# A macaron layer step on one core: FFN 1's first result tile kept in SBUF, the vector engine's setup and low parts in another order, and the samples' state products in four parts inside the tenth gate unit

## The chip, the cores and the metric

The kernel runs on one core of one Trainium2 chip. The metric is the device time of one launch in microseconds. The kernel before took 2427.97 us (median of 3 runs, 2427.48 to 2428.36).

## The reference, cut to what matters

One decoder layer step for 1024 prompt tokens and 8 sample tokens (1032 columns in all), all in float32, model width 1024:

```
x = x + 0.5 * (silu(n1 @ W_gate) * (n1 @ W_up)) @ W_down     # FFN 1, n1 = rmsnorm(x), inner width 2816
proj  = rmsnorm(x) @ w_in            # RWKV features | S5 input u | 2048 columns of gates
y_a   = rwkv7(features, state)       # matrix-state recurrence, 8 heads of 64
y_b   = s5(u, state)                 # bu = ug @ bb; x_t = ab * x_{t-1} + bu_t; y = x @ C + D * u; GELU; GLU
x = x + (sigmoid(g_a) * (y_a @ w_a_up) + sigmoid(g_b) * (y_b @ w_b_up)) @ w_out
x = x + 0.5 * FFN 2(rmsnorm(x));  outputs: rmsnorm(x), last features, RWKV and S5 states
```

## The kernel before

All activations lie with the model width on the 128 partitions and the 1032 tokens along the free axis, in 8 tiles. Every float32 operand of a large product is split into a high part (`whi`, `b11_hi`, ...) and a low part (`wlo`, ...), and a product is three matmuls, high by high, high by low and low by high.

**FFN 1, first half.** The inner width 2816 is 22 tiles of 128 rows. Gate and up of one tile together are a *pair* (`NP` = 22, numbered 0 to 21). A pair is done as seven Strassen products, n = 0 to 6, of 24 matmuls each (4 weight tiles, 3 parts, 2 column blocks of 258) on the seven operands b11, t1, t2, b21, t3, b22, t4, which stay in SBUF (L939 for a pair, L902 for one product). ScalarE (ACT) makes the high parts of the weights (L749) and copies some products out of PSUM (L849, L855, L861); GpSimd (POOL) makes sums of weight parts (L504) and the low parts (L501); VectorE (DVE) adds, scales by `rstd` and multiplies (L663 to L686). The last DVE step of a pair (named `a2`, L686; L644 for pairs 0 and 1) leaves the pair's result, a *tile* of 128 x 1032, in `gate[:, j]`, j = pair mod 2. SyncE (SP) then stores it to DRAM (`spill`, L414).

PE waits in each pair for a few of these steps: product 2 for ACT's first copy (`p1`), product 5 for ACT's third copy (`p5`, L861), product 6 for DVE's `u2a` (L668); and every product for the low part of its weights (`st_lo`, L501).

**FFN 1, second half ("down").** 4 blocks of tiles (0 to 5, 6 to 11, 12 to 17, 18 to 21) times 8 output tiles are 32 *units* of up to 54 matmuls of 344 columns (L983). A unit needs the high and low parts of its block's result tiles. These go through 18 *slots* of SBUF (`g.slot`), most of which overlap the seven operands and so come free only when a product of the last pair has read its operand for the last time. SP brings a tile back (`a_back`, L457), ACT makes its high part (`tile_high`, L830), DVE its low part (`tile_low`, L651). Slot 15, that of tile 0, lies over x's last two rows, which are used up after pair 0. Unit 0 is done in two pieces: tiles 0 to 2 when DVE's `g2a` of pair 21 is there (L675), tiles 3 to 5 when `u1` is there (L681). DVE adds the first piece at L696, and each unit at L703; PE's unit u waits until unit u - 2 has been added. POOL splits the weights of each unit (L542, L544).

All engines run their own instruction streams in order: an instruction that waits holds up all that stand behind it on that engine. SP's queue is in order too: `spill(20)`, `a_back(0)`, weights of units 0 and 1, `a_back(1)` to `a_back(5)` (each pair of them behind a product of pair 21), 8 loads of x, `spill(21)`, weights of unit 2, `a_back(6)` and so on.

**The S5 setup.** DVE computes the S5 tables in the gaps: a generator of some 600 small instructions (`s5_setup_dve`, L1122 on), of which `spend` (L1256) issues a share behind each pair (slot number below 22, nominally 4700 ns) and behind each down unit (slot 22 + u, nominally 2700 ns). Four table parts (`turn`) come first, then short instructions on 128 x 16 values, then the parts `in` and `out`. ACT stores a finished part in a later slot.

**The projection stage.** 16 gate units (L206, 8 weight tiles of 9 matmuls of 344 columns) have the S5 products between them: `to_state` (L1873), `out` (L1903, L1907), and after gate unit 8 `samples` (L1884), 64 matmuls of 8 columns in one run.

Of the kernel before, what the change touches and what calls it, by code (L numbers as in the profile page):

```python
# [15 lines left out]
NB = 8  # L16
TOK = SEQ + NB
DT = D // P
# [329 lines left out]
def first_ffn(nc, g, w_up, w_down, gcol, gnext, x_in, x_rows, consts_in, s5_in, a_dram, x_dram, setup, ahead, block):  # L348
# [6 lines left out]
    spilled = [16, 16]  # L355
# [51 lines left out]
    def _(sp):  # L407
# [31 lines left out]
        spill(0, 0, 0)  # L439
# [24 lines left out]
        a_back(0, 15)  # L464
# [84 lines left out]
    def _(v):  # L549
# [86 lines left out]
        for j in range(2):  # L636
# [7 lines left out]
            on(v.tensor_tensor(gate, gate, up, ALU.mult))  # L644
# [9 lines left out]
        for pair in range(2, NP):  # L654
# [3 lines left out]
            if last:  # L658
                for t in range(4):
                    tile_low(t)  # L660
# [7 lines left out]
            on(v.tensor_tensor(U[1], two("x", j), U[1], ALU.add))  # L668
            g.fst_up.wait(v, 0, pair, "u2a")
            on(v.tensor_tensor(U[1], U[1], R[1], ALU.mult))  # L670
            if last:
                tile_low(4)
# [5 lines left out]
            if last:  # L678
                tile_low(5)
            done(v, 0, pair, 6)  # L680
            on(v.tensor_tensor(U[0], two("x", j), R[0], ALU.mult))  # L681
            g.fst_up.wait(v, 0, pair, "u1")
# [3 lines left out]
            on(v.tensor_tensor(G[1], G[1], U[1], ALU.mult))  # L686
            if not last:
                setup["vector"](pair, PAIR_NS)
                assert pair < NP - 2 or setup["tables"]() == 4
        for u in range(len(FIRST_BLOCKS) * DT):  # L690
            b, k = divmod(u, DT)
            xd = blocks(g.xd[:, k, :])
            if u == 0:
                v.wait_ge(g.x_in[0], 32)
                v.wait_ge(g.m_half, 1)
                v.scalar_tensor_tensor(xd, g.ps[:, 5:8, 0:BLK], 0.5, xd, ALU.mult, ALU.add).then_inc(g.set_free[1], 1)  # L696
# [19 lines left out]
    def _(act):  # L716
# [109 lines left out]
        def tile_high(t):  # L826
            b, k = divmod(t, 6)
            act.wait_ge(g.a_in[t % 6], 16 + 16 * (t // 6 + 1))
# [3 lines left out]
        for pair in range(2, NP):  # L832
# [15 lines left out]
            act.wait_ge(g.a_out[j], spilled[j] + 16 * (pair // 2))  # L848
# [24 lines left out]
            if pair == NP - 2:  # L873
                tile_high(0)
# [376 lines left out]
def s5_setup(g, s5_dram):  # L1251
# [294 lines left out]
def s5_block(nc, g, w_gate, w_glu, w_b, gate_dram, wb_dram, o_dram, cs_dram, x0_in, y_dram, ys_dram, s5p_out, s5s_out,  # L1546
# [25 lines left out]
    if block:  # L1572
# [280 lines left out]
        def _(pe):  # L1853
# [3 lines left out]
            def gate(k):  # L1857
                product(pe, g, 0, 0, u0 + k, DT, k % 2, use[k % 2] + k // 2, 0, hi, lo, None, inside.get(k))
# [18 lines left out]
            def samples(y_turns):  # L1877
                pe.wait_ge(g.v_free, 4)
                pe.wait_ge(g.y_set, 2 * y_turns)
                for n in range(2):  # L1880
                    for j in range(J):
                        for q in range(2):
                            c = (n * J + j) * NB
                            last = pe.matmul(g.ps[rows(q), 6, c:c + NB], g.G8[:, j, n, rows(q)],  # L1884
# [2378 lines left out]
```

## Time and profile before

| | |
|---|---|
| profiled execution | 2429.68 us, span 2427.9 us, TensorE clock 0.992 of full speed |
| PE busy | 2367.0 us (97%) |
| DVE, POOL, ACT busy | 1390.5, 1186.2, 711.5 us |
| DMA | 243.89 MB, mean 100 GB/s |

PE is at work nearly all the time. The span in 40 slices of some 61 us shows where it is not: in the first slice, in the eighth (`PE ...9 8...`, `PEld ...7...`, from 425 us), around slices 21 to 26, where the recurrence runs, and in the last one. The chain that ended last reaches back only to 1573.65 us and is 32% PE; before that the order of the stages is told by PE's own idle times. "PEld" is the weight load of TensorE, which overlaps the matmuls. The clock column of the window view is the granted TensorE clock, 1.00 being 2.4 GHz.

### The profile page before, as it was taken

How to read it: one execution, taken by the hardware profiler on the slowest of the kernel's cores; microseconds unless marked ns; L12 is line 12 of the kernel's file. 1: busy time of each engine (PE TensorE's matmuls, PEld its weight loads, DVE VectorE, ACT ScalarE, POOL GpSimd, SP SyncE). 2: the span in 40 equal slices, each digit the busy share in tenths (PEclk: the TensorE clock that was granted, in tenths of full speed). 3: DMA queues.
4: the chain of work that ended last, by engine and by line, in shares of the span. 5: the costliest groups of instructions: out<-in, count | busy, mean ns of one | idle time of the engine just before them, and what ended most of it. 6: DMA issues, size and time to landing. Idle time of an engine off the chain costs nothing. (4 is left out here: it accounts for less than half of the span.)

```text
span 2427.9 us, 51909 instructions
## 1 busy us (share of the span) xinstructions
PE 2367.0 (97%) x21964; PEld 2310.3 (95%) x21964; DVE 1390.5 (57%) x2023; ACT 711.5 (29%) x1349; POOL 1186.2 (49%) x750
## 2 busy tenths in 40 slices
PE   8999999899999999999989999999999999999997
PEld 8999999799999999999988888899999999999997
DVE  6666666788545455652566676576844444453225
ACT  6333333311020000111437666312433333341001
POOL 3868686634434345322330000254777777765640
PEclk9999999999999999999999999999999999999999
DMA  5212121344333523634360110172222222153212
GB/s 215 94 63 94 70 104 70 139 171 133 99 104 136 114 88 108 153 86 129 131 203 18 34 33 4 50 260 87 79 87 76 79 74 81 61 196 95 82 46 71
DMA packets 104135, 243.89 MB, mean 100 GB/s; under 512 B 17240, under 2 KB 43480, under 8 KB 103328
## 3 DMA queue, kind: packets, MB, share of 16 engines
q1 hardware_dynamic: 76560, 190.72, 23.8%
q10 hardware_dynamic: 27408, 50.76, 6.6%
q8 instruction: 126, 2.06, 0.4%
q14 instruction: 41, 0.34, 0.1%
HBM read 174.47 MB, written 65.82 MB: 99 GB/s over the span
## 5 line engine op out<-in xcount | busy, mean ns | idle before, releaser
L172 POOL TENSOR_TENSOR whi<-wraw,small 128x1024 fp32r<-128x1024 f32 (+1 forms) x60 | 103.3, 1721 | 417.2 <-PE ps L206 340.7
L206 PE MATMUL ps<-hhi,whi 128*128 128x344 f32 x816 | 176.9, 325 | 0.0
L206 PE MATMUL ps<-hlo,whi 128*128 128x344 f32 x816 | 173.1, 320 | 0.0
L206 PE MATMUL ps<-hhi,wlo 128*128 128x344 f32 x816 | 172.8, 320 | 0.0
L909 PE MATMUL ps<-t_hi,whi 128*128 128x258 f32 x672 | 138.1, 287 | 12.3 <-POOL wlo L501 5.7
L175 POOL TENSOR_TENSOR wlo<-wraw,whi 128x1024 fp32r<-128x1024 f32 (+1 forms) x60 | 145.5, 2424 | 4.7
L3939 PE MATMUL ps<-t_hi,whi 128*128 128x258 f32 x704 | 143.6, 285 | 3.1 <-ACT ffn_gate L3846 1.0
L3939 PE MATMUL ps<-t_lo,whi 128*128 128x258 f32 x704 | 142.1, 283 | 0.0
L3939 PE MATMUL ps<-t_hi,wlo 128*128 128x258 f32 x704 | 141.2, 282 | 0.0
L206 PEld LDWEIGHTS ps<-hhi,whi 128*128 128x128 f32 x816 | 136.3, 189 | 2.1 <-issue 0.7
L206 PEld LDWEIGHTS ps<-hlo,whi 128*128 128x128 f32 x816 | 137.9, 189 | 0.0
L909 PE MATMUL ps<-t_lo,whi 128*128 128x258 f32 x672 | 137.2, 286 | 0.0
L206 PEld LDWEIGHTS ps<-hhi,wlo 128*128 128x128 f32 x816 | 136.7, 188 | 0.0
L909 PE MATMUL ps<-t_hi,wlo 128*128 128x258 f32 x672 | 136.4, 285 | 0.0
L2218 POOL TENSOR_TENSOR sm_v<-sm_v,rw_e 128x2048 f32<-128x2048 f32 x1 | 3.6, 3622 | 256.1 <-DVEq L1981 256.1
L909 PE MATMUL ps<-b_hi,whi 128*128 128x258 f32 x576 | 117.5, 286 | 8.7 <-DVE b_lo L561 8.7
L909 PEld LDWEIGHTS ps<-t_hi,whi 128*128 128x128 f32 x672 | 105.2, 192 | 15.1 <-POOL wlo L501 8.6
L3622 POOL TENSOR_TENSOR wlo<-weights_sum,whi 128x512 fp32r<-128x512 f32 x66 | 92.3, 1399 | 52.5 <-ACT whi L3818 51.3
L909 PE MATMUL ps<-b_lo,whi 128*128 128x258 f32 x576 | 116.8, 284 | 0.0
L501 POOL TENSOR_TENSOR wlo<-weights_sum,whi 128x512 fp32r<-128x512 f32 x60 | 86.0, 1433 | 63.1 <-ACT whi L749 62.4
L909 PE MATMUL ps<-b_hi,wlo 128*128 128x258 f32 x576 | 116.1, 283 | 0.0
L983 PE MATMUL ps<-a_hi,whi 128*128 128x344 f32 x528 | 112.0, 320 | 1.7 <-issue 1.5
(592 smaller groups left out, 6823.9 us busy)
## 6 DMA issues: line engine op xcount, KB each, us to landing
weights_raw_b<-ffn_up SPq DMA_DIRECT2D x22, 1024.0 KB, 5.0
wraw<-ffn_up SPq DMA_DIRECT2D x21, 1024.0 KB, 5.0
a_spilled<-ffn_gate SPq DMA_DIRECT2D x40, 516.0 KB, 2.7
a_raw<-a_spilled SPq DMA_DIRECT2D x40, 516.0 KB, 4.3
wraw<-ffn_down SPq DMA_DIRECT2D x48, 384.0 KB, 3.2
wraw<-w_mix SPq DMA_DIRECT2D x18, 512.0 KB, 3.6
gates<-gate_out ACTq DMA_DIRECT2D x16, 516.0 KB, 3.5
wraw<-w_gates SPq DMA_DIRECT2D x16, 512.0 KB, 3.9
```

The source lines that it names most:

```text
L172: pool.tensor_tensor(g.whi[:, s, 0:n], g.wraw[:, s, 0:n], g.zero.to_broadcast([P, n]), ALU.add).then_inc(g.w_hi, 1)
L175: pool.tensor_tensor(g.wlo[:, s, 0:n], g.wraw[:, s, 0:n], g.whi[:, s, 0:n].bitcast(F32), ALU.subtract).then_inc(g.w_split, 1)
L206: last = pe.matmul(g.ps[:, 3 * bank_set + b, 0:BLK], w[:, s, k * P:(k + 1) * P], x(k, b), start=(k == 0 and first), stop=(k == kt - 1 and ...
L501: pool.tensor_tensor(ring(g.wlo, n), source(n), ring(g.whi, n).bitcast(F32), ALU.subtract).then_inc(g.st_lo, 1)
L909: last = pe.matmul(g.ps[:, b0 + c, 0:QB], w(k), x[:, k, c * QB:(c + 1) * QB], start=start and k == 0 and fresh, stop=k == DT // 2 - 1 and ...
L983: last = pe.matmul(g.ps[:, b0 + c, 0:BLK], w[:, s, n * P:(n + 1) * P], x[:, c * BLK:(c + 1) * BLK], start=n == tiles[0] and fresh, stop=n ...
L2218: st.do(pool.tensor_tensor(V, V, over(E7[:, :, sample]), ALU.mult))
L3622: pool.tensor_tensor(ring(g.wlo, n), source(n), ring(g.whi, n).bitcast(F32), ALU.subtract).then_inc(g.st_lo, 1)
L3939: last = pe.matmul(g.ps[:, b0 + c, 0:QB], ring(w, r, k), x[:, k, c * QB:(c + 1) * QB], start=start and k == 0 and first, stop=k == DT // 2 ...
```

## The change

1. **Tile 0 stays in SBUF.** Pair 0's last multiply (L644) writes straight into slot 15 instead of `gate[:, 0]`, after waiting that the first operands and `t4`'s low part are made. `spill(0)` and `a_back(0)` are gone. ACT makes the tile's high part after pair 3 instead of after pair 20, DVE its low part after pair 4 instead of in pair 21. ACT's first copy in pair 2 waits for pair 0's last multiply instead of for the spill.
2. **Low parts in pair 21.** DVE made tiles 0 to 3 ahead of the pair's steps, 4 after `u2m`, 5 after `g2m`. Now it makes 1 and 2 ahead, 3 between `u2a` and `u2m`, and 4 and 5 after `u1`, followed by the addition of unit 0's first piece, which stood behind the pair's two last multiplies.
3. **Setup.** `spend` stops in the pairs once the four table parts are done (after pair 18), and goes on in the down units.
4. **Samples.** The 64 small matmuls are issued 16 at a time behind weight tiles 0 to 3 of gate unit 9 instead of all behind unit 8.

```diff
@@ first_ffn, SP
-        spill(0, 0, 0)
         spill(0, 0, 1)
...
-        a_back(0, 15)
@@ first_ffn, DVE
-            on(v.tensor_tensor(gate, gate, up, ALU.mult))
+            if j == 0:
+                v.wait_ge(g.b_hi, HI0)
+                v.wait_ge(g.t4_lo, 4)
+                on(v.tensor_tensor(g.slot[15][2][:, :], gate, up, ALU.mult))
+            else:
+                on(v.tensor_tensor(gate, gate, up, ALU.mult))
...
             if last:
-                for t in range(4):
-                    tile_low(t)
+                tile_low(1)
+                tile_low(2)
...
+            if pair == 4:
+                tile_low(0)
@@ first_ffn, ACT
-            act.wait_ge(g.a_out[j], spilled[j] + 16 * (pair // 2))
+            if pair == 2:
+                g.fst_up.wait(act, 0, 0, "a2")
+            else:
+                act.wait_ge(g.a_out[j], spilled[j] + 16 * (pair // 2))
...
-            if pair == NP - 2:
+            if pair == 3:
                 tile_high(0)
@@ s5_setup
     def spend(slot, ns):
+        if slot < NP and len(ready) == 4:
+            return
...
                 ready.append(slot)
+                if slot < NP and len(ready) == 4:
+                    return
@@ gate units, PE
-            def samples(y_turns):
+            def samples(k):
+                if k >= 4:
+                    return
+                if k == 0:
+                    pe.wait_ge(g.v_free, 4)
+                    pe.wait_ge(g.y_set, 2 * 6)
+                for x in range(2 * J // 4 * k, 2 * J // 4 * (k + 1)):
+                    n, j = divmod(x, J)
...
+                if k == 3:
+                    last.then_inc(g.v_done, 1)
```

The rest of the diff counts semaphores anew, one spill and one load fewer.

ACT at the turn from pair 20 to pair 21, before. `a_hi_212` is the high part in slot 15 (tile 0), `a_raw_214` the tile as loaded, L844 the silu, L749 the weights' high parts, L849 the first copy:

```order
L844 ACTIVATE ffn_gate<-ffn_gate 128x516
L830 ACTIVATE a_hi_212<-a_raw_214 128x1032
L749 ACTIVATE whi<-weights_sum 128x512
L849 ACTIVATE ffn_gate<-ps 128x516
L749 ACTIVATE whi<-weights_raw_b 128x512
L855 ACTIVATE ffn_up<-ps 128x516
```

The same place after (L854 the silu, L756 the high parts, L862, L868 and L874 the three copies, L840 `tile_high`; `a_hi_167` and `a_hi_170` are tiles 1 and 2):

```order
L854 ACTIVATE ffn_gate<-ffn_gate 128x516
L756 ACTIVATE whi<-weights_sum 128x512
L862 ACTIVATE ffn_gate<-ps 128x516
L756 ACTIVATE whi<-weights_raw_b 128x512
L868 ACTIVATE ffn_up<-ps 128x516
L756 ACTIVATE whi<-weights_raw_b 128x512
L840 ACTIVATE a_hi_167<-a_raw_169 128x1032
L840 ACTIVATE a_hi_170<-a_raw_172 128x1032
L874 ACTIVATE ffn_gate<-ps 128x516
L756 ACTIVATE whi<-weights_sum 128x512
```

Tile 0 no longer stands between pair 20's silu and pair 21's weights; tiles 1 and 2 stand, as before, between pair 21's second and third copy.

DVE in pair 21, before (L651 `tile_low`, L663 to L681 the pair's steps):

```order
L651 TENSOR_TENSOR a_lo_213<-a_raw_214,a_hi_212 128x1032
L651 TENSOR_TENSOR a_lo_168<-a_raw_169,a_hi_167 128x1032
L651 TENSOR_TENSOR a_lo_171<-a_raw_172,a_hi_170 128x1032
L651 TENSOR_TENSOR a_lo_174<-a_raw_175,a_hi_173 128x1032
L663 TENSOR_TENSOR ffn_gate<-ps,ffn_gate 128x516
L665 TENSOR_TENSOR ffn_gate<-ffn_gate,rstd 128x516
L668 TENSOR_TENSOR ffn_up<-ps,ffn_up 128x516
L670 TENSOR_TENSOR ffn_up<-ffn_up,rstd 128x516
L651 TENSOR_TENSOR a_lo_177<-a_raw_178,a_hi_176 128x1032
L675 TENSOR_TENSOR ffn_gate<-ps,ffn_gate 128x516
```

DVE at the turn from pair 20 to pair 21, after (L692 and L694 the two last multiplies of pair 20, L654 `tile_low`):

```order
L692 TENSOR_TENSOR ffn_gate<-ffn_gate,ffn_up 128x516
L694 TENSOR_TENSOR ffn_gate<-ffn_gate,ffn_up 128x516
L654 TENSOR_TENSOR a_lo_168<-a_raw_169,a_hi_167 128x1032
L654 TENSOR_TENSOR a_lo_171<-a_raw_172,a_hi_170 128x1032
L666 TENSOR_TENSOR ffn_gate<-ps,ffn_gate 128x516
```

No setup instruction stands behind pair 20 any more, and two low parts instead of four stand ahead of pair 21's steps.

PE around gate unit 9, before (L206 a gate unit's matmuls, L1884 the samples):

```order
L206 MATMUL ps<-hhi,wlo 128x344 x3
L1884 MATMUL ps<-s_u,s_to_state 64x8 x64
L206 MATMUL ps<-hhi,whi 128x344 x3
L206 MATMUL ps<-hlo,whi 128x344 x3
L206 MATMUL ps<-hhi,wlo 128x344 x3
```

After (L1904 the samples):

```order
L1904 MATMUL ps<-s_u,s_to_state 64x8 x16
L206 MATMUL ps<-hhi,whi 128x344 x3
L206 MATMUL ps<-hlo,whi 128x344 x3
L206 MATMUL ps<-hhi,wlo 128x344 x3
L1904 MATMUL ps<-s_u,s_to_state 64x8 x16
```

The run of 64 has become four runs of 16 with 9 large matmuls between them.

## Rows read from the trace of the kernel before

**Rows 1.** Windows: us, busy time (instructions) by engine, granted clock, DMA.

```profile
300.00:420.00 120.00, 119.70 (x993) 119.08 (x993) 80.92 (x166) 41.46 (x72) 92.12 (x66) 1.00 0.24 88
...
465.30:470.60 5.30, 5.28 (x24) 5.28 (x25) 3.50 (x2) 1.99 (x3) 5.30 (x3) 0.50 0.44 181
...
1092.20:1095.60 3.40, 3.40 (x16) 3.38 (x15) 2.38 (x6) 0.00 (x0) 0.65 (x1) 0.52 0.77 238
```

**Rows 2.** Timeline, PE, FFN 1's last two pairs: start, length, instruction, idle before.

```profile
449.22 0.51 PE L909 MATMUL ps<-t_hi,whi 128*128 128x258 f32 x2 [3.81 <-DVE ffn_up L668]
...
465.32 0.80 PE L909 MATMUL ps<-t_hi,whi 128*128 128x258 f32 x2 [5.67 <-POOL wlo L501]
...
484.60 0.71 PE L983 MATMUL ps<-a_hi,whi 128*128 128x344 f32 x3 [1.52 <-issue]
```

**Rows 3.** Timeline, DVE: end of pair 18, setup behind pair 19.

```profile
409.50 0.69 DVE L686 TENSOR_TENSOR ffn_gate<-ffn_gate,ffn_up 128x516 f32<-128x516 f32 x1
...
432.32 1.27 DVE L1177 TENSOR_TENSOR s_par<-vec 128x16 f32<-128x16 f32 x1
...
446.85 0.17 DVE L1199 TENSOR_SCALAR s_par<-s_par 128x16 f32<-128x16 f32 x1
```

**Rows 4.** Timeline, ACT: the high parts of tiles 0, 1 and 2.

```profile
461.73 1.06 ACT L830 ACTIVATE a_hi<-a_raw 128x1032 fp32r<-128x1032 f32 x1 [9.46 <-DMA a_raw<-a_spilled]
462.70 0.61 ACT L749 ACTIVATE whi<-weights_sum 128x512 fp32r<-128x512 f32 x1
...
465.23 2.07 ACT L830 ACTIVATE a_hi<-a_raw 128x1032 fp32r<-128x1032 f32 x2
```

**Rows 5.** Timeline, SP's queue (the length is from first to last).

```profile
432.57 23.74 SPq L414 DMA_DIRECT2D a_spilled<-ffn_gate  x2
456.41 0.40 SPq L457 DMA_DIRECT2D a_raw<-a_spilled  x1
...
458.18 15.94 SPq L457 DMA_DIRECT2D a_raw<-a_spilled  x5
```

**Rows 6.** Tile a_raw, 440 to 540 us: low parts in ns, loads to landing.

```profile
L651 DVE TENSOR_TENSOR a_lo<-a_raw,a_hi x11: 1223/1236/2889, 462.9 to 533.3; 128x1032 fp32r<-128x1032 f32 x11
...
DMA to landing us min/median/max: 3.4/5.6/8.7
```

**Rows 7.** Timeline, DVE: pair 21 and the first down units.

```profile
476.83 0.68 DVE L663 TENSOR_TENSOR ffn_gate<-ps,ffn_gate 128x516 f32<-128x516 f32 x1
...
490.44 1.23 DVE L696 SCALAR_TENSOR_TENSOR x_down<-ps,x_down 128x1032 f32<-128x1032 f32 x1
493.86 1.23 DVE L703 SCALAR_TENSOR_TENSOR x_down<-ps,x_down 128x1032 f32<-128x1032 f32 x1 [2.19 <-PE ps L983]
...
507.00 1.23 DVE L703 SCALAR_TENSOR_TENSOR x_down<-ps,x_down 128x1032 f32<-128x1032 f32 x1
```

**Rows 8.** Timeline, POOL: weights of units 0, 2 and 5 (5 waits for unit 3).

```profile
480.62 2.19 POOL L544 TENSOR_TENSOR wlo<-wraw,whi 128x768 fp32r<-128x768 f32 x1
...
497.59 1.85 POOL L544 TENSOR_TENSOR wlo<-wraw,whi 128x768 fp32r<-128x768 f32 x1
...
519.38 1.57 POOL L542 TENSOR_TENSOR whi<-wraw,small 128x768 fp32r<-128x768 f32 x1 [5.06 <-PE ps L983]
```

**Rows 9.** Timeline, PE: the samples between gate units 8 and 9.

```profile
1087.80 0.63 PE L206 MATMUL ps<-hhi,wlo 128*128 128x344 f32 x3
1088.36 3.99 PE L1884 MATMUL ps<-s_u,s_to_state 128*64 128x8 f32 x128
1092.28 1.23 PE L206 MATMUL ps<-hhi,whi 128*128 128x344 f32 x3
```

**Rows 10.** Page, part 5: POOL's low parts of the pairs' weights (mean ns).

```profile
L501 POOL TENSOR_TENSOR wlo<-weights_sum,whi 128x512 fp32r<-128x512 f32 x60 | 86.0, 1433 | 63.1 <-ACT whi L749 62.4
```

**Rows 11.** Timeline of pair 2, POOL and PE.

```profile
65.16 2.25 POOL L501 TENSOR_TENSOR wlo<-weights_sum,whi 128x512 fp32r<-128x512 f32 x1
...
67.52 0.48 PE L909 MATMUL ps<-t_hi,whi 128*128 128x258 f32 x2 [1.33 <-ACT ffn_gate L849]
```

More of the change, by code:

```diff
@@ L354, in first_ffn @@
     x_late = [*g.a_in, *g.a_out]
-    spilled = [16, 16]
+    spilled = [0, 16]
     def raw(par):
@@ L668, in _ @@
             on(v.tensor_tensor(U[1], two("x", j), U[1], ALU.add))
+            if last:
+                tile_low(3)
             g.fst_up.wait(v, 0, pair, "u2a")
             on(v.tensor_tensor(U[1], U[1], R[1], ALU.mult))
-            if last:
-                tile_low(4)
             done(v, 0, pair, 5)
@@ L677, in _ @@
             on(v.tensor_tensor(G[1], G[1], R[1], ALU.mult))
-            if last:
-                tile_low(5)
             done(v, 0, pair, 6)
             on(v.tensor_tensor(U[0], two("x", j), R[0], ALU.mult))
+            if last:
+                tile_low(4)
+                tile_low(5)
+                xd = blocks(g.xd[:, 0, :])
+                v.wait_ge(g.x_in[0], 32)
+                v.wait_ge(g.m_half, 1)
+                v.scalar_tensor_tensor(xd, g.ps[:, 5:8, 0:BLK], 0.5, xd, ALU.mult, ALU.add).then_inc(g.set_free[1], 1)
             g.fst_up.wait(v, 0, pair, "u1")
@@ L827, in tile_high @@
             b, k = divmod(t, 6)
-            act.wait_ge(g.a_in[t % 6], 16 + 16 * (t // 6 + 1))
+            if t == 0:
+                g.fst_up.wait(act, 0, 0, "a2")
+            else:
+                act.wait_ge(g.a_in[t % 6], 16 + 16 * (t // 6 + (t % 6 > 0)))
             hi, _, full = g.slot[FIRST_BLOCKS[b][2][k]]
@@ L847, in _ @@
             done(act, 0, pair, 0)
-            act.wait_ge(g.a_out[j], spilled[j] + 16 * (pair // 2))
+            if pair == 2:
+                g.fst_up.wait(act, 0, 0, "a2")
+            else:
+                act.wait_ge(g.a_out[j], spilled[j] + 16 * (pair // 2))
             on(act.activation(G[0], two("x", j), ACT.Copy))
@@ L1857, in gate @@
             def gate(k):
-                product(pe, g, 0, 0, u0 + k, DT, k % 2, use[k % 2] + k // 2, 0, hi, lo, None, inside.get(k))
+                product(pe, g, 0, 0, u0 + k, DT, k % 2, use[k % 2] + k // 2, 0, hi, lo, None, inside.get(k),
+                        samples if k == SAMPLE_UNIT else None)
             def to_state(p, y_turns):
@@ L1875, in to_state @@
                 last.then_inc(g.v_done, 1)
-            def samples(y_turns):
[L1878 to L1884, printed above, removed]
-                                             g.U8[:, 2 * j + q, NB + CH:CH + 2 * NB], start=True, stop=True)
-                last.then_inc(g.v_done, 1)
+            def samples(k):
[6 more added lines that the diff above has]
+                    n, j = divmod(x, J)
+                    for q in range(2):
+                        last = pe.matmul(g.ps[rows(q), 6, x * NB:x * NB + NB], g.G8[:, j, n, rows(q)],
+                                         g.U8[:, 2 * j + q, NB + CH:CH + 2 * NB], start=True, stop=True)
+                if k == 3:
+                    last.then_inc(g.v_done, 1)
             def out(p, w, states):
@@ L1912, in _ @@
                      4: [lambda: to_state(2, 2)], 5: [lambda: out(1, 0, 3)], 6: [lambda: to_state(3, 4)],
-                     7: [lambda: out(2, 0, 4)], 8: [lambda: samples(6)], 9: [lambda: out(3, 0, 5)]}
+                     7: [lambda: out(2, 0, 4)], 9: [lambda: out(3, 0, 5)]}
+            SAMPLE_UNIT = 9
             inside = {4 + 2 * p: (6, lambda p=p: out(p, 1, 0)) for p in range(4)}
@@ L3262 @@
 M0, S0, T0 = 16, 4, 4
-DONE0, IN0, OUT0 = 7 * NP, 8 * NP, 16 + 8 * NP
-BACK0 = [16 + 16 * len(range(r, FT, 6)) for r in range(6)]
+DONE0, IN0, OUT0 = 7 * NP, 8 * NP, (8 * NP, 16 + 8 * NP)
+BACK0 = [16 * (r > 0) + 16 * len(range(r, FT, 6)) for r in range(6)]
 SPILLED = NP - KEPT
@@ L3842, in body @@
                 if b < 10 and (b or j >= 2):
-                    act.wait_ge(g.a_out[j], i * 16 + (OUT0 + 16 * b))
+                    act.wait_ge(g.a_out[j], i * 16 + (OUT0[j] + 16 * b))
                 if b == 10:
```

5 lines of the change are left out of this document (1 added, 4 removed).

## The prediction

> **What bounds the kernel now.** I read the page's busy times and its 40 slices first: PE is busy 97% of the span, so only PE's idle or slowed time can be won, and the change can pay only where PE waits today. The window view then gives two kinds of stretches. In a steady one PE is full: 993 matmuls in 120 us [rows 1], so one matmul takes 0.1208 us and a product of 24 takes 2.90 us. The turn from FFN 1's first half to its second is the other kind. PE's timeline [rows 2] shows it in one column, the idle time before an instruction. Product 6 of pair 20 starts at 449.22 after 3.81 us, so product 5 was over at 445.4; product 2 of pair 21 at 465.32 after 5.67 us, and the first down unit at 484.60 after 1.52 us. The clock adds to it: after each long idle time the granted clock is the lower level, 1.2 GHz; the 24 matmuls from 465.3 to 470.6 took 5.3 us at 0.50 [rows 1]. From 445.4 to 484.6 eight products were done; at 2.90 us each they need 23.2 us. The stretch lost 39.2 - 23.2 = 16.0 us, which is nearly all that this part of the change can win.
>
> Who was late? For the first stall, DVE: its setup behind pair 19 runs from 432.32 to 447.02 [rows 3], three times its nominal 4.7 us, and the step for which PE waits (L668) stands behind it. For the second, ACT: it sat 9.46 us in front of tile 0's high part [rows 4], with pair 21's weight split behind it, because SP could load tile 0 (456.41) only after its in-order `spill(20)` (the second of the two at 432.57, issued at its end, 456.31), which waited for the same late DVE [rows 5]. So both stalls have one root, DVE, and one amplifier, tile 0 in ACT's order.
>
> **The stretch after the change.** Without setup behind pair 19, DVE does its steps as products end, and both stalls go. Products then end back to back: pair 20's last at 448.3, pair 21's products 0 to 6 at 451.2, 454.1, 457.0, 459.9, 462.8, 465.7 and 468.6. What is late next has to be followed along each engine.
>
> *SP and the DMA.* Pair 18, whose DVE steps run without a delay, ends its last one at 410.19 [rows 3]. Its last product ended 14 products, 40.6 us, before pair 20's 448.3, at 407.7, so 2.5 us earlier. For pair 20 that gives 450.8. `spill(20)` goes then, the weights of units 0 and 1 by 452.0, `a_back(1)` and (2) at about 452.1 and 452.5, (3) and (4) at 454.2, (5) at 460.0. Tile 1 before: issued at 458.18, taken by ACT at 465.23 at once, so landed within 7.0 us [rows 4, 5], tile 2 a little later; both lie between the minimum and the maximum of 3.4 and 8.7 [rows 6]. One tile of 0.53 MB (tile 0) is gone from the queue ahead of them, 1.3 us at the 400 GB/s of a full queue. So tile 1 lands near 457.8 and tile 2 near 458.8.
>
> *ACT.* Its two high parts (2.07 for two [rows 4]) end near 459.8; its third copy, at the 0.6 of a piece of 512 columns (row at 462.70 [rows 4]), at 460.4, the weights of product 5, as long, at 461.0, POOL's low part (1.43 on average [rows 10]) at 462.4. PE wants product 5 at 462.8. This holds by 0.4 us only: I cost it at nothing and keep it as the first rival.
>
> *DVE.* Low parts of tiles 1 and 2 end between 461.5 and 462.3. From there to `g2a`, for which the first down unit waits, stand exactly the six instructions that stood there before, in another order: five steps and one low part. They took from 476.83 [rows 7] to just before PE's start at 484.60 [rows 2], 7.7 us, and the low part alone has the longest row of its kind, 2.89 [rows 6]. So the down stage starts at 462.0 + 7.7 = 469.7 at the middle. POOL's weights for unit 0 ended at 482.81 [rows 8], 6.4 us after product 4's end (470.6 plus two products, 476.4), so now at 469.2: not later than DVE.
>
> PE therefore starts down at 469.7 instead of 484.60: **14.9 us won**. Bounds: 16.0 if nothing is late; 11.4 if the loads land 3.5 us later than I say.
>
> The Trainium skill (page "SBUF — State Buffer", section "Who interferes with whom") says that a DVE instruction with two SBUF inputs and a GpSimd instruction that reads SBUF exclude each other for a whole instruction. The trace agrees: the same low part takes between 1.22 and 2.89 us [rows 6], the long ones while POOL worked. With no such exclusion the low part would take 1.23, DVE would not be the limit, and the sum would be 0.5 us better.
>
> **The down stage.** The two last multiplies of pair 21 now stand behind two low parts and the first addition. Before, that addition began 5.8 us after the start of down (490.44 [rows 7]) and the multiplies were over by then; now I get 8.5 us. `spill(21)`, the weights of unit 2 and `a_back(6)` are queued behind it on SP, 2.6 us later against PE. Unit 2's weights were ready at 499.44 [rows 8], 2.9 us before PE wanted them (unit 0 over at 493.8 [rows 7], one more of 8.5: 502.3), and the 8 loads of x, which crowded them, will have landed: I cost this at nothing, 0 to 1 us.
>
> The setup that is taken out of the pairs, 3 + 27 + 20 instructions, comes behind the units: slots 0 to 2 now hold some 15 short ones each. A unit takes 8.5 us (unit 0 over at 493.8 [rows 7], unit 3 at 519.3 [rows 8]); DVE has an addition of 1.23, a low part of 1.23 to 2.9, and 15 instructions of 0.2 us, of which about three may wait for POOL's 3.4 us per unit: 5.5 to 9 us. Unit 1's addition ran from 507.00 to 508.2 [rows 7], 2.6 us before PE needed its banks at 510.8 (two units after 493.8). In the sum nothing; it is the second rival. The setup then ends four units later, near unit 21, before DVE gets its second job in the last block.
>
> In unit 0 an idle time of 0.17 us goes: 0.1.
>
> **Pair 2.** ACT's wait for the spill is replaced by one for a multiply that ends earlier. PE idled 1.33 us there, but POOL's low part for the same product ended at 67.41, 0.1 us before PE started [rows 11]. Won: 0.1, bounds 0 and 1.3. The high and low part of tile 0 (1.06 and 1.23 us) fall into pairs 3 and 4, in which ACT and DVE have idle time and PE has none.
>
> **Samples.** 128 recorded small matmuls take from 1088.36 to 1092.28 [rows 9], and the 3.4 us behind them run at 0.52 of the clock [rows 1]. At full clock that work takes 1.8, so 1.6 us can be won if the clock stays up. Each change between small and large costs: three large ones issued from 1087.80 take 0.48, so 0.1 goes by until 1088.36; for coming out, where a full weight load follows a short matmul, I estimate twice that. Three more of each are 0.8 us. Net 0.8 won. No row shows small and large ones mixed like this, so bounds are 1.6 won and 1.4 lost (the clock falls all the same, and the changes cost twice as much). DVE's wait for the result moves into a gap of 10 us.
>
> **Sum:** 14.9 + 0.1 + 0.1 + 0.8 = 15.9 us. The profiled execution took 2429.68 us (span 2427.9 and 1.8 around it): 2413.8. The median shown, 2427.97, is 1.7 lower, so I predict 2412.1.
>
> **Rivals.** *ACT still stands in front of a load.* Tiles 1 and 2 land as late as the latest load before, 8.7 us after issue: 461.2, so product 5 waits some 2 us; if the stall grows to 3 or 4 us, the lower clock costs another 1.5 to 2.5, as at 465. The total gain is then 10 to 12: 2416 to 2418, say 2417. For it: 0.4 us of margin. Against it: a shorter queue.
>
> *Setup crowds the units.* Behind pair 19, 27 instructions took 14.7 us, 0.54 each [rows 3]. If the 15 short ones of a slot do the same, a unit costs DVE 8.1 + 2.5 to 4.1 = 10.6 to 12.2 us against 8.5; over three units 6 to 11, less the 2.6 of slack: 3.5 to 8.5 us of stalls. Then 2415.5 to 2420.5, say 2418. Against it: POOL works 3.4 us of 8.5 there, and worked nearly always behind pair 19.
>
> *The same, and slower than before.* If each of the short ones waits for one POOL instruction, 1.2 us as at 432.32 [rows 3], a slot costs 20.5 us, three of them 61.5 against 25.5: 33 us lost after slack, and the time is about 2445. Slower begins where a short one costs more than 0.82 us on average ((25.5 + 2.6 + 16) / 3 = 14.7 for a slot, less 2.5, over 15).
>
> *The samples lose.* The clock falls and the changes cost double: 2.2 us worse than forecast, 2414.3. This is inside the forecast's own range.
>
> **How the numbers follow.** Forecast (own range 2410 to 2415.5) 0.62; ACT behind a load 0.17; crowded units, mildly 0.10; both or more, ending near no change, 0.06; slower 0.05. For 8 in 10: 2409.5 to 2419. The lower end is all bounds at once, 16.0 + 0.1 + 1.3 + 1.6 = 19 us, slightly cut. A change under 0.2% (4.9 us) can't be told from none. Faster by more 0.89, within 0.06, slower 0.05.
>
> **What would show it.** In the new trace PE has no idle time between 430 and 468 us and keeps the full clock; one short wait for DVE's `g2a` before the first down unit near 469.7; ACT's idle time before its first high part in pair 21 under 4 us. Behind the samples the clock stays at 2.4 GHz and unit 9 ends 0.8 us earlier against unit 8's end. I am wrong if PE waits for POOL's weights at product 5, or for DVE's additions in units 3 to 5.

## The result, and the profile after

The changed kernel takes 2415.76 us (median of 5 runs, 2415.53 to 2417.57) against 2428.36 for the kernel before (5 runs, 2427.48 to 2429.63): ratio 0.9949, 95% interval 0.9936 to 0.9962, 12.6 us less. The forecast was 2412.1, with a range of 2409.5 to 2419 for 8 in 10; its narrower range, 2410 to 2415.5, was missed by 0.3 us. One of the 19 runs of the kernel before beside the first experiments took 8030.62 us and does not count in their ratios. The profiled executions are 14.1 us apart, 2429.68 and 2415.58.

Where these 14.1 us come from is read from one kind of event, DVE's reads of finished units and gate tiles, which both traces have: how much earlier does each come? At 50 us it is 0.2 us already, before anything that the change touches has a part in it; at the first down unit 12.60 (read on PE); in DVE's addition of unit 0 12.99, and again 12.99 from unit 8 to 968 us; at gate unit 4 of the projection 13.67; at unit 9 14.34; at the end 14.1. The additions of units 1 to 7 come only 9.4 to 12.4 us earlier, since DVE runs behind there, but PE is not held up by it. So 12.4 us were won at the turn (12.60 less the 0.2) and 0.4 in unit 0. Another 0.7 appeared in the first gate units, where the change does nothing, and 0.67 at the samples.

The windows of the changed kernel (columns as in [rows 1]) show a steady stretch as full as before, the turn without a slow clock, and a stretch over the second and third of the samples' four parts:

```profile
300.00:420.00 120.00, 119.70 (x994) 119.08 (x993) 79.43 (x163) 41.28 (x72) 92.27 (x66) 1.00 0.25 88
430.00:459.00 29.00, 28.89 (x241) 28.69 (x240) 9.11 (x11) 9.47 (x17) 22.39 (x16) 1.00 0.31 111
461.60:464.60 3.00, 2.93 (x24) 2.93 (x25) 2.41 (x3) 2.37 (x3) 1.35 (x1) 1.00 0.34 125
1079.00:1082.60 3.60, 3.60 (x72) 3.35 (x69) 1.51 (x5) 0.00 (x0) 0.19 (x1) 1.00 0.80 256
```

PE's idle times at the turn, to be held against [rows 2]. The waits of 3.81 and 5.67 us are gone. A new one stands before product 4 of pair 21 (461.67), and the first down unit starts at 472.00:

```profile
461.67 0.51 PE L922 MATMUL ps<-t_hi,whi 128*128 128x258 f32 x2 [2.05 <-ACT ffn_gate L874]
467.88 0.51 PE L922 MATMUL ps<-t_hi,whi 128*128 128x258 f32 x2 [0.20 <-POOL wlo L499]
472.00 0.74 PE L996 MATMUL ps<-a_hi,whi 128*128 128x344 f32 x3 [0.96 <-POOL wlo L542]
```

ACT there ([rows 4] before), with L840 the high parts of tiles 1 and 2, L874 the third copy and L756 the weights of product 5:

```profile
458.71 1.06 ACT L840 ACTIVATE a_hi<-a_raw 128x1032 fp32r<-128x1032 f32 x1 [3.71 <-DMA a_raw<-a_spilled]
459.99 1.06 ACT L840 ACTIVATE a_hi<-a_raw 128x1032 fp32r<-128x1032 f32 x1 [0.21 <-DMA a_raw<-a_spilled]
460.96 0.58 ACT L874 ACTIVATE ffn_gate<-ps 128x516 f32<-128x516 f32 x1
461.44 0.62 ACT L756 ACTIVATE whi<-weights_sum 128x512 fp32r<-128x512 f32 x1
```

The copy ends at 461.54 and product 4 starts 0.13 later: PE waits for the copy, the copy stands behind two high parts, and these wait for a load. (The section on the kernel before has one of these waits wrong: in the code product 4 waits for ACT's third copy, L861 there, and product 5 for the second, L855, which is `p5`.) SP issued that load at 452.33 ([rows 5] before; SPq is SP's queue):

```profile
450.63 0.35 SPq L414 DMA_DIRECT2D a_spilled<-ffn_gate  x1
451.16 1.12 SPq L451 DMA_DIRECT2D wraw<-ffn_down  x2
452.33 7.65 SPq L456 DMA_DIRECT2D a_raw<-a_spilled  x5
```

DVE was not what the first down unit waited for. Its `g2a` is the L678 here, over at 468.98, while POOL's weights (whi L540, wlo L542; [rows 8] before) ended at 471.95:

```profile
465.45 1.22 DVE L654 TENSOR_TENSOR a_lo<-a_raw,a_hi 128x1032 fp32r<-128x1032 f32 x1
466.59 1.78 DVE L675 TENSOR_TENSOR ffn_up<-ffn_up,rstd 128x516 f32<-128x516 f32 x1
468.30 0.68 DVE L678 TENSOR_TENSOR ffn_gate<-ps,ffn_gate 128x516 f32<-128x516 f32 x1
```

```profile
465.55 2.27 POOL L499 TENSOR_TENSOR wlo<-weights_raw_b,whi 128x512 fp32r<-128x512 f32 x1 [2.07 <-ACT whi L756]
467.79 1.92 POOL L540 TENSOR_TENSOR whi<-wraw,small 128x768 fp32r<-128x768 f32 x1
469.79 2.16 POOL L542 TENSOR_TENSOR wlo<-wraw,whi 128x768 fp32r<-128x768 f32 x1
```

Behind the start of down DVE does the setup beside the additions of the units. The addition of unit 1 ([rows 7] before, 507.00) starts here:

```profile
494.84 1.23 DVE L710 SCALAR_TENSOR_TENSOR x_down<-ps,x_down 128x1032 f32<-128x1032 f32 x1
```

Unit 0 was over at 480.87 and a unit takes 8.49 us, so this is 5.5 us after unit 1's end (4.7 before), and 1.8 us before PE wants the banks for unit 3 (2.6 before).

In pair 2 nothing moved ([rows 11] before): PE still waits 1.33 us and starts 0.1 after POOL's low part for the same product, which ends at 67.26:

```profile
65.00 2.26 POOL L499 TENSOR_TENSOR wlo<-weights_sum,whi 128x512 fp32r<-128x512 f32 x1
```

### The profile page after: what moved, and what is told of

The parts are those of the page before. It is cut to its first block and busy times, and to the rows that moved or that the text cites. A ratio compares the mean times of both kernels' runs of the same rounds, so it can differ in the third digit from the quotient of the medians.

```text
span 2413.8 us, 51906 instructions
## 1 busy us (share of the span) xinstructions
PE 2361.9 (98%) x21964; PEld 2304.6 (95%) x21964; DVE 1387.9 (57%) x2023; ACT 711.8 (29%) x1349; POOL 1188.7 (49%) x750
## 5 line engine op out<-in xcount | busy, mean ns | idle before, releaser
L206 PE MATMUL ps<-hhi,whi 128*128 128x344 f32 x816 | 176.6, 325 | 0.0
L206 PE MATMUL ps<-hlo,whi 128*128 128x344 f32 x816 | 172.7, 320 | 0.0
L206 PE MATMUL ps<-hhi,wlo 128*128 128x344 f32 x816 | 172.4, 320 | 0.0
L206 PEld LDWEIGHTS ps<-hhi,whi 128*128 128x128 f32 x816 | 135.5, 188 | 2.1 <-issue 0.7
L206 PEld LDWEIGHTS ps<-hlo,whi 128*128 128x128 f32 x816 | 137.6, 189 | 0.0
L206 PEld LDWEIGHTS ps<-hhi,wlo 128*128 128x128 f32 x816 | 136.3, 188 | 0.0
L3644 POOL TENSOR_TENSOR wlo<-weights_sum,whi 128x512 fp32r<-128x512 f32 x66 | 92.4, 1399 | 52.5 <-ACT whi L3840 51.3
L996 PE MATMUL ps<-a_lo,whi 128*128 128x344 f32 x528 | 111.5, 319 | 0.0
```

The lines of the kernel that those rows point to most:

```text
L206: last = pe.matmul(g.ps[:, 3 * bank_set + b, 0:BLK], w[:, s, k * P:(k + 1) * P], x(k, b), start=(k == 0 and first), stop=(k == kt - 1 and ...
L996: last = pe.matmul(g.ps[:, b0 + c, 0:BLK], w[:, s, n * P:(n + 1) * P], x[:, c * BLK:(c + 1) * BLK], start=n == tiles[0] and fresh, stop=n ...
L3644: pool.tensor_tensor(ring(g.wlo, n), source(n), ring(g.whi, n).bitcast(F32), ALU.subtract).then_inc(g.st_lo, 1)
```

## The experiments

Each trace gives one execution. A single execution of a kernel varies by some 2 us, a median of five by some 1 us, so differences under 2 us are read from the start of the first down unit, and the times say only that nothing else went wrong. That start varies too, with the landing of the loads: in two traces with the changed kernel's code up to there and the clock at 1.00 it is at 472.00 and 471.31. In both it comes 13.29 us after ACT starts tile 1's high part (458.71 and 458.02), and this distance is the finer measure.

**Setup alone.** The kernel before, with `spend`'s two stops and nothing else.

```diff
     def spend(slot, ns):
+        if slot < NP and len(ready) == 4:
+            return
...
+                if slot < NP and len(ready) == 4:
+                    return
```

> The kernel before, with the setup stopped in the pairs and nothing else of the change. Theory (one root, DVE's setup, and one amplifier, tile 0 in ACT's order): the first stall (3.8 us before product 6 of pair 20) and its slow clock go, but SP still issues tile 0's load only behind spill(20), now near 451, so ACT stands in front of it until about 456.5 and product 2 of pair 21 starts near 459.5 after some 5 us of waiting, at half the clock. First down unit near 477 to 478, 6.5 to 8 us earlier than the 484.60 of before; time 6.5 to 8 us below before. Rival (the setup alone is the cause, the load fits once DVE is on time): no wait over 1 us in pair 21, first down unit near 472, 12 us or more won. Second rival (the setup crowds the down units): the start of down is earlier, but the shift against before shrinks by over 1 us between units 1 and 6.

2422.18 us (9 runs) against 2428.61 (19 runs), ratio 0.9976 (0.9966 to 0.9986). PE's two idle times, and ACT between them:

```profile
459.64 0.80 PE L909 MATMUL ps<-t_hi,whi 128*128 128x258 f32 x2 [5.56 <-POOL wlo L501]
477.90 0.71 PE L983 MATMUL ps<-a_hi,whi 128*128 128x344 f32 x3 [1.49 <-issue]
```

```profile
456.12 1.06 ACT L830 ACTIVATE a_hi<-a_raw 128x1032 fp32r<-128x1032 f32 x1 [8.35 <-DMA a_raw<-a_spilled]
```

The theory held in each number: first stall gone, ACT 8.35 us in front of tile 0's load, a stall of 5.56, first down unit at 477.90, 6.7 us earlier. The rival, by which the setup alone is the cause, is out. So is a part of the recorded explanation: with DVE on time the second stall is still 5.56 us of 5.67, so DVE's lateness was not its root. The crowding rival is out too: at 755 us the shift was 6.70, what it was at the start of down, though slots 0 to 2 held setup as in the changed kernel.

**Tile 0 alone.** The kernel before, with tile 0 written into slot 15, without `spill(0)` and `a_back(0)`; DVE's low parts 1, 2, 3 ahead, 4 and 5 as before.

```diff
-        spill(0, 0, 0)
-        a_back(0, 15)
...
+                on(v.tensor_tensor(g.slot[15][2][:, :], gate, up, ALU.mult))
```

> The kernel before, with tile 0 kept in SBUF and nothing else (setup, order of the low parts and samples as before). Theory: the first stall of 3.8 us before product 6 of pair 20 and its slow clock stay; the 5.67 us wait before product 2 of pair 21 goes, with the half clock behind it; product 4 waits about 1 us for ACT's third copy, which stands behind the loads of tiles 1 and 2. First down unit near 476.5, 8 us earlier; time about 8 us below before. Rival (tile 0 was only one of several things in ACT's way): tiles 1 and 2, issued after spill(20) at 456.3, hold ACT just as long; under 4 us won.

2419.93 us (5 runs) against 2428.61, ratio 0.9963 (0.9949 to 0.9976):

```profile
449.49 0.79 PE L920 MATMUL ps<-t_hi,whi 128*128 128x258 f32 x2 [3.83 <-DVE ffn_up L671]
467.68 0.51 PE L920 MATMUL ps<-t_hi,whi 128*128 128x258 f32 x2 [1.23 <-ACT ffn_gate L872]
477.78 0.74 PE L994 MATMUL ps<-a_hi,whi 128*128 128x344 f32 x3 [1.21 <-POOL wlo L542]
```

```profile
449.40:453.40 4.00, 3.91 (x18) 3.92 (x19) 2.44 (x3) 1.69 (x4) 3.26 (x3) 0.50 0.00 0
```

The first stall stays, with half the clock behind it, the second shrinks from 5.67 to 1.23 us. The first down unit comes 6.8 us earlier; I had said 8, since POOL's 1.21 us at the end were not in my sum. Two things follow. Setup and tile 0 are two causes that add up: 6.7 and 6.8 us alone, 12.6 together (all counted from 484.60), 0.9 less than the sum. And the wait for the third copy, the one that the prediction did not have before product 4, belongs to the loads of tiles 1 and 2: it is here without the rest of the change.

**Samples alone.** The kernel before, with the samples' products in four parts.

> The kernel before, with only the samples' products in four parts. Theory: the clock stays at 2.4 GHz behind the small products, and from unit 8's end to unit 9's end 0.67 us are won, as in the changed kernel's trace; time 0.5 to 0.9 us below before, no shift anywhere else. Rival (the 0.7 us that the changed kernel gained between gate units 1 and 4 belong to this edit): 1.3 to 1.6 us won. Rival (the gain seen there is chance): 0 +- 0.3.

2427.95 us (11 runs) against 2428.61, ratio 0.9998 (0.9989 to 1.0007). In the trace unit 9 comes 0.66 us earlier against unit 8, as in the changed kernel. But the two kernels of the runs above have the samples in one piece, and there unit 9 came 1.53 and 1.54 us earlier than in the trace of before. The clock is why. Behind that one piece, first with the setup alone, then with tile 0 alone (the stretch that answers to 1092.20:1095.60 in [rows 1]):

```profile
1085.50:1089.10 3.60, 3.60 (x27) 3.60 (x24) 2.38 (x6) 0.00 (x0) 0.64 (x1) 1.00 0.78 258
```

```profile
1084.80:1088.40 3.60, 3.60 (x25) 3.60 (x24) 2.34 (x6) 0.00 (x0) 0.60 (x1) 1.00 0.84 293
```

It stayed at 2.4 GHz, with 25 to 27 matmuls in 3.6 us against 17 in before's trace. So the one piece is 0.87 us quicker than four parts where the clock stays, and 0.67 slower where it falls.

**The kernel before again**, one execution, to see whether the fall belongs to the kernel.

> The kernel before once more, for the clock behind the samples' run. In three traces of kernels with that run in one piece the 3.5 us behind it were at 0.53 to 0.55 of the clock twice and at 1.00 in two others. Theory (it comes and goes with the execution): either may be seen here, and nothing else differs by over 0.5 us. Rival (it belongs to the kernel): 0.5 of the clock again, 3.4 to 3.6 us long.

2430.37 us. The clock fell again:

```profile
1092.60:1096.20 3.60, 3.60 (x20) 3.58 (x17) 2.51 (x6) 0.00 (x0) 0.77 (x1) 0.53 0.81 285
```

Two executions of one kernel agree, so this leaves it open. One thing it does show: between 945 and 1025 us it gained 0.58 us on the first execution of the very same kernel. The 0.7 us of the first gate units are therefore the execution's and not the change's. Elsewhere they were 0 (setup alone) to 0.7 (changed kernel again). The claim "nothing else differs by over 0.5" missed: behind the turn this execution was 1.1 us later, with ACT's tile 0 waiting 10.71 us where [rows 4] has 9.46.

**The samples in one piece, in the changed kernel.**

```diff
-                      7: [lambda: out(2, 0, 4)], 9: [lambda: out(3, 0, 5)]}
-            SAMPLE_UNIT = 9
+                      7: [lambda: out(2, 0, 4)], 8: [lambda: samples(6)], 9: [lambda: out(3, 0, 5)]}
```

> The changed kernel with the samples' products in one run behind gate unit 8 again. The traces of the first two single-part kernels kept the full clock behind that run, without the edit, and were 0.85 us quicker there than the four parts. Theory (the slow clock behind the run comes and goes with the execution): if the clock stays at 1.00 behind the run, unit 9 ends 0.85 us earlier against unit 8's end than in the changed kernel, if it falls 0.67 us later; the median of the runs is within 1 us of the changed kernel's. Rival (the run always pulls the clock down where the stages before it are as in the kernel before or after): 0.67 us slower, at 0.5 of the clock behind the run.

2415.77 us (5 runs; the changed kernel on the same chip 2415.29; before 2428.70). In the trace the clock fell, and the shift did not grow from unit 8 to unit 9:

```profile
1078.20:1081.70 3.50, 3.50 (x15) 3.50 (x14) 2.32 (x6) 0.00 (x0) 0.58 (x1) 0.53 0.89 299
```

One piece: three traces with a fall (the kernel before twice, this one), two without (setup alone, tile 0 alone), in kernels that differ only 600 us earlier. No kernel was seen both ways, so the rival, that the fall belongs to what runs before, is not out; more traces of one kernel would settle it. Behind four parts the clock stayed at 1.00 in all eight traces that have them. The medians, 0.5 us apart, can't be told from each other.

**The changed kernel again.**

> The changed kernel once more, beside its variants on one chip. Theory: first down unit near 472.0, product 4 of pair 21 waits 2.05 us for ACT's third copy, as in its first trace; median within 1 us of 2415.8. What an execution gives at random is seen from how its trace differs from the first one's.

2415.29 us (5 runs, 2413.28 to 2417.64), ratio 0.9945 (0.9932 to 0.9959). The wait before product 4 was 1.74 us, but the down stage began at 473.36, 1.36 later than in the first trace, since this time the clock fell behind the stall. Its windows, to be held against 461.60:464.60 above:

```profile
461.50:464.50 3.00, 2.98 (x17) 2.99 (x18) 2.35 (x3) 2.32 (x3) 1.34 (x1) 0.66 0.39 154
464.50:467.50 3.00, 3.00 (x22) 3.00 (x21) 1.29 (x2) 1.29 (x3) 0.58 (x1) 0.77 0.00 0
```

**The third copy first.** In the changed kernel ACT's third copy goes ahead of the high parts of tiles 1 and 2.

```diff
             hi(2)
+            done(act, 0, pair, 2)
+            on(act.activation(G[1], two("x", j), ACT.Copy))
             if pair == NP - 1:
                 tile_high(1)
                 tile_high(2)
-            done(act, 0, pair, 2)
-            on(act.activation(G[1], two("x", j), ACT.Copy))
```

> The changed kernel, with ACT's third copy of pair 21 ahead of the high parts of tiles 1 and 2 instead of behind them. Theory (product 4 waits for that copy, and the copy waits behind a load): the 2.05 us wait before product 4 is gone; the weights of product 5 still stand behind the two high parts, so product 5 waits 0.5 to 1 us, and POOL's chain to unit 0's weights ends near 470.3. First down unit near 470.3 instead of 472.00; time 1.3 to 2 us below the changed kernel. Rival (the two loads themselves bound the stretch, whatever stands behind them): first down unit at 471.7 or later, under 0.4 us won.

2413.84 us (5 runs), ratio to before 0.9936 (0.9923 to 0.9950):

```profile
463.75 0.51 PE L922 MATMUL ps<-b_hi,whi 128*128 128x258 f32 x2 [0.87 <-POOL wlo L499]
470.43 0.74 PE L996 MATMUL ps<-a_hi,whi 128*128 128x344 f32 x3 [0.64 <-POOL wlo L542]
```

The stall before product 4 is gone, product 5 waits 0.87, and the first down unit is 1.57 us earlier than in the changed kernel's first trace. The loads landed 0.2 later than there (tile 1's high part at 458.92): from that row to the start of down it is 11.51 us instead of 13.29, so the copy's place is worth 1.8 us. This is the direct test of the failed step below.

**The low parts back.** The changed kernel with DVE's low parts 3, 4, 5 and the first piece's addition in the places of before.

> The changed kernel with the low parts of tiles 3, 4 and 5 and the addition of unit 0's first piece where they stood in the kernel before. Theory (POOL's weights bound the start of down, not DVE): first down unit within 0.5 us of 472.0, time within 0.7 us of the changed kernel; a short wait for u1 or a low part at unit 0's second piece at most. Rival (DVE bounds it, as the prediction had it): the start of down moves by over 1 us.

2414.39 us (5 runs), ratio 0.9947. First down unit at 471.37 with product 4 at 461.27, 10.10 us apart; 10.33 in the changed kernel. So part 2 of the change is worth nothing at the turn, or 0.2 us less than nothing, and POOL is the limit there:

```profile
471.37 0.74 PE L994 MATMUL ps<-a_hi,whi 128*128 128x344 f32 x3 [1.21 <-POOL wlo L542]
```

**Loads and copy first.** In the changed kernel SP issues tiles 1 and 2 ahead of the weights, and ACT's order in pair 21 is third copy, `tile_high(1)`, weights of product 5, `tile_high(2)` and `(3)`, weights of product 6, `tile_high(4)`.

```diff
-        weights(0)
-        weights(1)
         for k, tiles in ((0, (1, 2)), (1, (3, 4)), (3, (5,))):
...
+            if k == 0:
+                weights(0)
+                weights(1)
```

> The changed kernel with SP issuing tiles 1 and 2 ahead of the weights of units 0 and 1, and ACT in the order third copy, high part 1, weights of product 5, high parts 2 and 3, weights of product 6, high part 4. Theory (only what stands in front of a load or behind a high part was late): tile 1's high part starts at 457.6 instead of 458.7, no wait before products 4, 5 and 6 of pair 21, and POOL's chain behind the low part for product 6 (1.4 to 2.3, then 1.9 and 2.2 us) ends at 468.9 to 469.7; first down unit there, 1.0 us over the moved copy alone and 2.5 to 3 us earlier than in the changed kernel. Rival (DVE's g2a takes POOL's place): first down unit at 470.4 or later, PE waiting for DVE.

2412.98 us (5 runs), ratio 0.9938 (0.9924 to 0.9951). The load landed in time, at 457.36 or earlier (ACT took it without idle time). But the first down unit came at 470.55, no earlier than with the copy alone. The rival was right; DVE, with `g2a` (L679), and POOL beside it:

```profile
465.70 1.89 DVE L655 TENSOR_TENSOR a_lo<-a_raw,a_hi 128x1032 fp32r<-128x1032 f32 x1
467.51 2.33 DVE L676 TENSOR_TENSOR ffn_up<-ffn_up,rstd 128x516 f32<-128x516 f32 x1
469.76 0.68 DVE L679 TENSOR_TENSOR ffn_gate<-ps,ffn_gate 128x516 f32<-128x516 f32 x1
```

```profile
464.58 1.92 POOL L541 TENSOR_TENSOR whi<-wraw,small 128x768 fp32r<-128x768 f32 x1
466.57 2.72 POOL L543 TENSOR_TENSOR wlo<-wraw,whi 128x768 fp32r<-128x768 f32 x1
```

POOL, now earlier, ends at 469.29, and DVE's multiply of 0.70 us takes 2.33 beside it: `g2a` ends at 470.44.

**Low part 3 behind `g2a`.** As that kernel, with the high parts of tiles 1 and 2 together (what each of the two edits is worth is not separated) and

```diff
-            if last:
-                tile_low(3)
             g.fst_up.wait(v, 0, pair, "u2a")
...
             on(v.tensor_tensor(G[1], two("z", j), G[1], ALU.add))
+            if last:
+                tile_low(3)
```

> The kernel with both loads and the third copy first, with the high part of tile 2 right behind that of tile 1 and DVE's low part of tile 3, which only unit 0's second piece needs, behind g2a instead of ahead of u2m. Theory (there DVE took POOL's place: the low part, 1.89 us, and the multiply, 2.33 us, both drawn out while POOL worked, stood in front of g2a): no wait before product 6, g2a over by 466.6, and PE waits for POOL's wlo of unit 0; first down unit at 468.9 to 469.4 instead of 470.55, 1.2 to 1.6 us won over that kernel. Rival (the steps themselves are slow, whatever their order): first down unit at 470 or later.

2412.79 us (5 runs, 2411.29 to 2414.36) against 2428.49, ratio 0.9935 (0.9921 to 0.9949), the lowest median of all. The interval overlaps the changed kernel's (0.9936 to 0.9962) by half, so that this version is better than it rests on the trace:

```profile
465.60 0.69 DVE L677 TENSOR_TENSOR ffn_gate<-ps,ffn_gate 128x516 f32<-128x516 f32 x1 [0.33 <-PE ps L924]
466.21 1.48 DVE L655 TENSOR_TENSOR a_lo<-a_raw,a_hi 128x1032 fp32r<-128x1032 f32 x1
```

```profile
469.42 0.74 PE L998 MATMUL ps<-a_hi,whi 128*128 128x344 f32 x3 [0.99 <-POOL wlo L543]
```

`g2a` ends 4.15 us sooner, no wait of PE is left in pair 21, and the first down unit comes 2.58 us earlier than in the changed kernel's first trace (1.13 over the kernel just before; 1.2 was the least expected). It waits for POOL again.

**POOL's split in the gap.** The same, with unit 0's weights split between the low parts for products 4 and 5 of pair 21.

```diff
             lo(i, b, n + 4)
+            if split_at is not None:
+                split(0)
             lo(i, b, n + 5)
```

> The same, with POOL's split of unit 0's weights between the low parts for products 4 and 5 of pair 21, where POOL is idle for over 4 us, instead of behind all low parts. Theory (what bounds the start of down is then PE alone): no wait over 0.2 us before products 4 to 6, first down unit at 468.3 to 468.7, 3.3 to 3.7 us earlier than in the changed kernel; median near 2412. Rival (the split comes before the weights have landed, or delays the low part for product 5): a wait of over 0.5 us before product 5.

2414.40 us (5 runs), ratio 0.9941. It missed, and the rival was right: POOL idled for the weights, which now stand behind two tiles in SP's queue, and its low part for product 5 came late by them:

```profile
459.05 2.20 POOL L511 TENSOR_TENSOR whi<-wraw,small 128x768 fp32r<-128x768 f32 x1 [2.37 <-DMA wraw<-ffn_down]
461.32 2.70 POOL L513 TENSOR_TENSOR wlo<-wraw,whi 128x768 fp32r<-128x768 f32 x1
463.98 1.74 POOL L500 TENSOR_TENSOR wlo<-weights_sum,whi 128x512 fp32r<-128x512 f32 x1
```

```profile
465.77 0.51 PE L931 MATMUL ps<-b_hi,whi 128*128 128x258 f32 x2 [2.96 <-POOL wlo L500]
```

A gap of 4 us on an engine is no room for 4 us of work if its data arrive in the middle. And here the second rival of the prediction, the crowded units, came true for a little. DVE's addition of unit 1 ran from 496.27 to 497.50, 7.4 us behind the unit's end, and PE's unit 3, which by the code waits for it, idled:

```profile
497.61 0.71 PE L1005 MATMUL ps<-a_hi,whi 128*128 128x344 f32 x3 [0.21 <-issue]
```

The shift against before falls from 13.47 in unit 0 to 12.90 at 968 us: 0.6 us lost in the units.

**Samples in two parts**, on top of that kernel.

> The same as the kernel with POOL's split in the gap, with the samples' products in two parts behind weight tiles 0 and 1 of gate unit 9 instead of four behind tiles 0 to 3. Theory (a change between small and large products costs 0.28 us, three more of them 0.85): two changes fewer win 0.5 to 0.6 us from unit 8's end to unit 9's end if the clock stays at 1.00. Rival (32 small ones in a row pull the clock down): half the clock behind a part and about 1 us lost.

From unit 8 to unit 9 the trace gained 1.26 us against before, four parts 0.67: two changes fewer are worth 0.59, as expected, and the clock stayed up. The median, 2417.66 us (5 runs, ratio 0.9953), is 3 us worse than without this edit. Its cause is not known. In the trace the clock fell behind the same stall before product 5 (2.97 us), and the down stage began at 473.02 against 471.65:

```profile
465.80:468.80 3.00, 3.00 (x16) 3.00 (x17) 0.33 (x1) 0.25 (x1) 1.47 (x1) 0.54 0.00 0
```

But the profiled execution, 2414.71 us at a mean clock of 0.995, is the fastest of the five; the other four ran at 0.993 and 0.994, those without the edit at 0.994 and 0.995. So the clock was lower somewhere in them, and no trace shows where. Whether two parts let the clock fall in some executions stays open.

## Why the prediction was right, and what in it was wrong

**The two causes: right; how they hang together: wrong.** DVE's setup made the first stall and tile 0 in ACT's order the second; each alone gives half (6.7 and 6.8 us). The prediction had "one root, DVE, and one amplifier". But with the setup gone the second stall stayed at 5.56 us of 5.67, and with tile 0 gone the first stayed (3.83 us, before 3.81). Tile 0's load stood behind `spill(20)` whether DVE was late or not. The forecast did not suffer from this, as the change removes both. PE ran without idle time and at the full clock up to 459.6; forecast was up to 468. ACT's idle time before its first high part was 3.71 us, under the 4 that was said.

**The turn: 12.4 us instead of 14.9.** The step that failed is ACT's: "Its two high parts end near 459.8; its third copy ... at 460.4 ... PE wants product 5 at 462.8. This holds by 0.4 us only". The margin was measured at the wrong product. The third copy frees the banks of product 4, which PE wants at 459.9; product 5 needs the second copy. With the forecast's own landing times that is 0.5 us of stall. The loads then landed 0.9 us later than said (tile 1 at 458.7, not 457.8); ACT waited 0.2 more for tile 2, PE was 0.3 earlier than said at product 4 (459.6, not 459.9), and the handover took 0.1: together the 2.05 us in the trace. Moving the copy gives 1.8 of them back. The first rival, ACT in front of a load, thus came partly true: with a stall of its 2 us, though before product 4, and, in the execution of the second trace, with its slow clock too. "PE waits for POOL's weights at product 5", the sign of being wrong, did not come.

**The limit before the first down unit: wrong engine.** The prediction had DVE end at 469.7 and POOL at 469.2. DVE ended at 468.98, with the shortest row for the low part (1.22) instead of the longest (2.89), and POOL at 471.95: its chain starts with product 4's end, which came 1.8 us late, and its low part took 2.27 us, not the 1.28 of the kernel before. With the loads and the copy first, POOL ended at 469.29 and DVE at 470.44, and the roles were changed; with one low part fewer in front of `g2a` they changed back (469.36 and 466.29). The two ends lay 1.1 to 3.1 us apart in these traces, and which is last hangs on an order that draws out one or the other.

**Setup in the down units: right at nothing, by a smaller margin than said.** PE has no idle time in the units, and the shift is 12.99 in unit 0 and from unit 8 on. The mild rival (3.5 to 8.5 us) and the one that ends slower (33 us) are out for this kernel. But DVE's additions came up to 5.6 us behind the units (4.8 before), and of the 2.6 us of slack 1.7 were left. With POOL's split in the gap nothing was left, and 0.6 us were lost: whoever makes the turn earlier still has this limit next. The addition of unit 0's first piece came 4.6 us after the start of down, not 8.5, and the weights were ready in time. In unit 0 itself 0.4 was won instead of 0.1.

**Pair 2: 0, said 0.1.** POOL's low part is the limit, as argued.

**Samples: 0.67, said 0.8, but only against a fall of the clock.** The price of a change between small and large products was rightly put: 0.87 for three. What the prediction took for granted is that the clock falls behind the one piece. It did in both traces of the kernel before and in one of the changed kernel with one piece, but not with the setup alone or tile 0 alone. Where it falls the edit gives 0.67 us, where it stays it costs 0.87; an estimate with three falls of five is 0.05 us. The runs with the edit alone (ratio 0.9998) can't tell its gain from zero.

**The sum.** 15.9 forecast against 14.1 in the pair of traces: 2.5 too much at the turn, 0.1 each at pair 2 and the samples, 0.3 too little in unit 0, and 0.7 that the execution gave by chance. The medians differ by 12.6, 3.3 less than forecast; 2.5 of these are the turn. The 1.5 us between that and the pair of traces are within what executions of one kernel differ by (2413.3 to 2417.6 for the changed one).

## What to carry to other kernels

For every instruction that is queued behind a load, write down which instruction of the busiest engine waits for it, and take that from the waits in the code, name by name; a margin against the next-but-one product is no margin. When a stall is removed, list the ends of all engines before the next joint, each with its shortest and its longest row: any of them that can be last is the limit in some order, and moving one changes the others' durations. Write down the slack that is left behind the joint too (here DVE's additions): an earlier start uses it up. A gain that rests on the clock falling in one trace needs a second trace before it is counted.

## What the runs showed of the hardware

- Behind an idle time of middle length the clock falls or stays by the execution. Before product 4 it stayed behind 2.05 us and fell behind 1.74 in two executions of one kernel, and stayed behind 1.23, 1.44 and 1.69; before product 5 it stayed behind 2.96 and fell behind 2.97, with the same instructions ahead. Behind 3.81 to 6.07 us it fell in all eight cases. A fall costs about 1.5 us (from product 4 to down 11.84 against 10.33). Behind the run of 64 small matmuls the 3.5 us were at 0.52 to 0.55 in three traces and at 1.00 in two, but there no kernel was seen both ways. The Trainium skill (page "TensorE: Matmul & The Clock Gate", section "What's actually happening") says of the start of a kernel that the number of slow matmuls varies from run to run; these traces show a change from run to run in the middle of one, behind the idle times.
- A DVE multiply of 128x516 with both inputs in SBUF took 0.69 us alone and 2.33 beside a POOL instruction of 2.72; its steps with one input in PSUM stayed at 0.68 to 0.70. POOL's low parts of 128x512 took between 1.28 and 2.27 at the turn. The one that started second was drawn out: in the changed kernel DVE's low part started at 465.45 and took 1.22, POOL's started 0.1 later and took 2.27; two more traces show the same pair of times.
- Two executions of one kernel differ by up to 0.7 us in places where nothing waits for anything that was changed, here between 945 and 1025 us. What is under that is told by local differences, not by the span.
